# Projections of K, V, Q and gate as fills between the attention tiles of each head, with a lookahead of two tiles in place of three

## What is computed

```python
s = jnp.einsum('bqhd,bkhd->bhqk', qi, k).astype(jnp.float32) * scale
s = s + ci[..., :, None] - cum[:, :, None, :]          # cum = cumsum(log_sigmoid(f))
s = jnp.where(k_pos[None, :] <= pi[:, None], s, NEG_INF)
p = jax.nn.softmax(s, axis=-1).astype(v.dtype)
o = jnp.einsum('bhqk,bkhd->bqhd', p, v)                # prompt; o_fox
...
y_fox = jnp.einsum('btc,cd->btd', o_fox * jax.nn.silu(g_fox), w_fox_out)
```

## Time and profile before

| | |
|---|---|
| median of 2 runs | 4568.74 us |
| the two runs | 4312.99 and 4824.48 us |
| the profiled execution, its own time | 4312.71 us |
| its span on the slowest core | 4311.1 us |
| spans of the eight cores | 4266.9 to 4311.1 us |
| mean granted TensorE clock of the cores | 0.936 to 0.940 |
| TensorE busy | 3636.3 us, 84% |
| VectorE, ScalarE, GpSimd busy | 832.6, 990.1, 806.7 us |

### The profile page before, as it was taken

How to read it: one execution, slowest core, us unless ns; L and a number is a source line. 1 busy time by engine, 2 the same in 40 slices (tenths; PEclk the granted TensorE clock), 3 DMA queues, 4 the chain that set the end, 5 groups by cost and what they waited for, 6 DMA issues and landing times.

```text
span 4311.1 us, 57458 instructions; the slowest of 8 cores (4266.9 to 4311.1 us)
## 1 busy us (share of the span) xinstructions
PE 3636.3 (84%) x20854; PEld 1846.9 (43%) x20854; DVE 832.6 (19%) x1331; ACT 990.1 (23%) x1808; POOL 806.7 (19%) x695
## 2 busy tenths in 40 slices
PE   3888888888888799988999996799958887888598
PEld 2555555555554344433444443344423333333243
DVE  1122222222222211111111111011101112111155
ACT  1344444444444411111111110011111221111011
POOL 1111111111111100001322232122211102222233
PEclk9999999999999899998999998899969998999799
DMA  6533333333333144435244444655492105655853
GB/s 91 70 55 55 51 49 52 51 55 55 55 51 51 20 80 79 86 59 42 27 38 40 40 40 2 103 118 118 109 151 38 20 1 102 131 126 132 172 157 122
DMA packets 500442, 311.75 MB, mean 72 GB/s; under 512 B 275440, under 2 KB 449264, under 8 KB 494140
## 3 DMA queue, kind: packets, MB, share of 16 engines
q0 software_dynamic: 354640, 143.19, 30.1%
q1 hardware_dynamic: 145528, 164.89, 13.8%
HBM read 353.68 MB, written 97.53 MB: 105 GB/s over the span
## 4 chain that ended last, share of the span: by engine, by line
PE 65%; DMA 17%; ACT 5%; issue 4%; POOL 4%; DVE 3%; SPq 1%; DVEq 0%; ACTq 0%; POOLq 0%
PE bank L153 64%; DMA pv<-m_scr 10%; POOL mt L182 3%; ACT pt L170 2%; DMA wm<-w_merge 2%; ACT rl L170 1%; DVE mrl L903 1%; DVE st L192 1%; DMA mwb<-w_mem_kv 1%; SPq L161 1%; DMA xb<-xp 1%; DMA cwb<-w_in 1%; DMA mT<-m_scr 1%; PE bank L157 1%; DMA mwb<-w_in 1%
## 5 line engine op out<-in xcount | busy, mean ns | idle before, releaser
L153 PE MATMUL bank<-xT,wm 128*128 128x512 bf16 (+1 forms) x3840 | 742.1, 347 | 102.0 <-DMA wm<-w_merge 102.0
L153 PE MATMUL bank<-xT,cwb 128*128 128x512 bf16 (+1 forms) x3840 | 693.1, 343 | 44.5 <-DMA cwb<-w_in 36.6
L153 PEld LDWEIGHTS bank<-xT,wm 128*128 128x128 bf16 x3840 | 330.7, 99 | 478.7 <-issue 126.8
L153 PEld LDWEIGHTS bank<-xT,cwb 128*128 128x128 bf16 x3840 | 324.4, 98 | 413.3 <-issue 54.8
L192 DVE SCALAR_TENSOR_TENSOR st<-bank,cqb 128x512 f32<-128x512 f32 (+5 forms) x588 | 295.0, 535 | 908.5 <-PE bank L153 871.8
L153 PE MATMUL bank<-wbuf,xT 128*128 128x256 bf16 (+1 forms) x3264 | 389.6, 283 | 16.4 <-ACT kv L176 16.4
L170 ACT ACTIVATE gt<-bank,bm 128x512 f32<-128x512 f32 (+1 forms) x240 | 147.0, 613 | 1061.7 <-PE bank L153 891.8
L182 DVE TENSOR_TENSOR mt<-bank,gt 128x512 f32<-128x512 f32 (+1 forms) x240 | 143.6, 598 | 1187.4 <-PE bank L153 598.8
L153 PE MATMUL bank<-xT,wbuf 128*128 128x512 bf16 (+1 forms) x1920 | 348.5, 342 | 18.0 <-ACT kT L176 8.5
L153 PEld LDWEIGHTS bank<-wbuf,xT 128*128 128x128 bf16 (+1 forms) x3264 | 330.3, 102 | 70.2 <-issue 21.7
L170 ACT ACTIVATE pt<-st,ncc 128x512 bf16<-128x512 f32 (+5 forms) x588 | 321.8, 594 | 144.0 <-DVE st L192 104.9
(11 more groups left out here) (131 smaller groups left out, 2468.9 us busy)
## 6 DMA issues: line engine op xcount, KB each, us to landing
m_scr<-mt SPq DMA_DIRECT2D x192, 256.0 KB, 2.0
pv<-m_scr SPq DMA_DIRECT2D x128, 256.0 KB, 3.0
wbuf<-w_in POOLq DMA_DIRECT2D x48, 512.0 KB, 12.0
wm<-w_merge POOLq DMA_DIRECT2D x24, 1024.0 KB, 15.1
cwb<-w_in POOLq DMA_DIRECT2D x48, 512.0 KB, 12.6
x<-xp SPq DMA_DIRECT2D x16, 1024.0 KB, 9.2
y_p<-rr SPq DMA_DIRECT2D x16, 1024.0 KB, 5.9
cqb<-cum_scr SPq DMA_DIRECT2D x12, 1024.0 KB, 5.1
```

What stands on the lines that cost most here:

```text
L153: return lambda e: e.matmul(out, lhsT=lhsT, rhs=rhs, start=start, stop=stop)
```

## The change

The projection work of a head is cut into closures: `kv_chunk`, `kv_finish` (casts and stores), `ktrans`, `proj_fm` (Q or gate of one block) and `cache_kT`. For each of the five token blocks there is a list of them in the order K/V chunks, finish, Q, gate, K transpose; the fifth also has the two cache transposes. `issue_S(i)` first emits all that is left of its own block's list, then S, the scale-and-add and Exp, and then one closure of the next block's list (two while in block 0). So block 0's list is emitted in one piece at the head's start, block 1's behind t0 to t3, block 2's behind t4 to t11, block 3's behind t12 to t19, block 4's behind t24 to t30. `load_w(h + 1)` is emitted when block 4's list is empty, behind t30. The lookahead goes from 3 to 2. The score ring has the banks 2, 3, 0 instead of 2, 3, 0, 1, and projections and transposes still alternate between banks 1 and 0.

```diff
+    SRING3 = [2, 3, 0]
+    pjb = [1]
+
+    def next_pj():
+        bk = pjb[0]
+        pjb[0] ^= 1
+        return bk
+
...
-        pending_kt = []
-        for grp in range(5):
-            chunks = [(tc, TCH[tc]) for tc in range(grp * 4, min(grp * 4 + 4, 17))]
-            s = grp % 2
-            for j, (tc, (t0, tn)) in enumerate(chunks):
-                bk = pj[0]; pj[0] ^= 1
+        def kv_chunk(grp, j, tc):
+            def f():
+                t0, tn = TCH[tc]
+                s = grp % 2
+                bk = next_pj()
                 for c in range(16):
-                    S.add(PE, MM(banks[bk][0:tn, 0:256], xT[:, c, t0:t0 + tn],
-                                 wbuf[:, c, 128:384], c == 0, c == 15),
+                    S.add(PE, MM(banks[bk][0:tn, 0:256], xT[:, c, t0:t0 + tn], wbuf[:, c, 128:384], c == 0, c == 15),
                           reads=[r_w[1], r_xT[tc]], writes=[bankr[bk]])
-                S.add(ACT, COPY(kv32[s][0:tn, j, :], banks[bk][0:tn, 0:256]),
-                      reads=[bankr[bk]], writes=[r_kv32[s]])
-            nj = len(chunks)
-            tn = chunks[0][1][1]
-            t0 = chunks[0][1][0]
...
-            def ktrans(grp=grp, s=s, nj=nj, tn=tn, t0=t0):
-                bk = pj[0]; pj[0] ^= 1
+                S.add(ACT, COPY(kv32[s][0:tn, j, :], banks[bk][0:tn, 0:256]), reads=[bankr[bk]], writes=[r_kv32[s]])
...
+        def ktrans(grp):
+            def f():
+                s = grp % 2
+                nj = min(4, 17 - grp * 4)
+                t0, tn = TCH[grp * 4]
+                bk = next_pj()
                 bv = banks[bk].bitcast(BF16)
                 for j in range(nj):
                     S.add(PE, TR(bv[:, j * 128:j * 128 + tn], kb[s][0:tn, j, :], identb[0:tn, 0:tn]),
                           reads=[r_kb[s], r_const], writes=[bankr[bk]])
                 S.add(ACT, COPY(kT[:, t0:t0 + nj * tn], bv[:, 0:nj * 128] if tn == 128 else bv[:, 0:tn]),
                       reads=[bankr[bk]], writes=[r_kT[grp]])
-            if pending_kt:
-                pending_kt.pop()()
-            pending_kt.append(ktrans)
-        for comp, dst, rr, slot in ((0, qT, r_qT, 0), (3, sg, r_sg, 2)):
-            for tb, (t0, tn) in enumerate(TBLK):
-                if tb == 1 and pending_kt:
-                    pending_kt.pop()()
-                bk = pj[0]; pj[0] ^= 1
+            return f
...
+        def proj_fm(comp, tb):
+            def f():
+                t0, tn = TBLK[tb]
+                slot = 0 if comp == 0 else 2
+                bk = next_pj()
...
-        if h + 1 < nheads:
-            load_w(h + 1)
-        for half in range(2):
-            bk = pj[0]; pj[0] ^= 1
-            bv = banks[bk].bitcast(BF16)
-            for j in range(4):
...
+        def cache_kT(half):
+            def f():
+                bk = next_pj()
+                bv = banks[bk].bitcast(BF16)
+                for j in range(4):
...
+        fq = {}
+        for b_ in range(5):
+            q_ = []
+            for j, tc in enumerate(range(b_ * 4, min(b_ * 4 + 4, 17))):
+                q_.append(kv_chunk(b_, j, tc))
+            q_.append(kv_finish(b_))
+            q_.append(proj_fm(0, b_))
+            q_.append(proj_fm(3, b_))
+            q_.append(ktrans(b_))
+            fq[b_] = q_
+        fq[4] += [cache_kT(0), cache_kT(1)]
+        wl = [False]
+
+        def pop_fill(b_, n):
+            if b_ not in fq:
+                return
+            for _ in range(n):
+                if fq[b_]:
+                    fq[b_].pop(0)()
+            if b_ == 4 and not fq[4] and not wl[0]:
+                wl[0] = True
+                if h + 1 < nheads:
+                    load_w(h + 1)
...
-        LA = 3
+        LA = 2
         slots = {}
...
-            sb_ = SRING[sbk[0] % 4]; sbk[0] += 1
+            pop_fill(tbidx, 99)
+            sb_ = SRING3[sbk[0] % 3]; sbk[0] += 1
...
             S.add(ACT, ACTF(pt[p][0:kn, n0:qn], stmp[st][0:kn, n0:qn], AF.Exp, bias=bias),
                   reads=[r_st[st], r_ncc], writes=[r_pt[p]])
+            pop_fill(tbidx + 1, 2 if tbidx == 0 else 1)
...
             if i + LA < nt_:
                 issue_S(i + LA)
             issue_PV(i)
+        for b_ in range(5):
+            pop_fill(b_, 99)
         if h + 1 < nheads:
             load_cache(h + 1)
             load_cqb(h + 1)
```

More of the change, by code:

```diff
@@ L516, in ktrans, with kv_finish @@
-            def ktrans(grp=grp, s=s, nj=nj, tn=tn, t0=t0):
-                bk = pj[0]; pj[0] ^= 1
+                S.add(ACT, COPY(kv32[s][0:tn, j, :], banks[bk][0:tn, 0:256]), reads=[bankr[bk]], writes=[r_kv32[s]])
+            return f
+        def kv_finish(grp):
+            def f():
+                s = grp % 2
+                nj = min(4, 17 - grp * 4)
+                t0, tn = TCH[grp * 4]
+                S.add(POOL, COPY(kb[s][0:tn, 0:nj, :], kv32[s][0:tn, 0:nj, 0:128]), reads=[r_kv32[s]], writes=[r_kb[s]])
+                S.add(POOL, COPY(vb[0:tn, grp * 4:grp * 4 + nj, :], kv32[s][0:tn, 0:nj, 128:256]),
+                      reads=[r_kv32[s]], writes=[r_vb[grp]])
+                if grp < 4:
+                    S.add(SP, DMA(O["fk_p"][t0:t0 + 512, h * 128:(h + 1) * 128].rearrange("(c p) n -> p c n", p=128),
+                                  kv32[s][:, :, 0:128]), reads=[r_kv32[s]], dmasem=d_kvo[s])
+                    S.add(SP, DMA(O["fv_p"][t0:t0 + 512, h * 128:(h + 1) * 128].rearrange("(c p) n -> p c n", p=128),
+                                  kv32[s][:, :, 128:256]), reads=[r_kv32[s]], dmasem=d_kvo[s])
+                else:
+                    S.add(SP, DMA(O["fk_s"][:, h * 128:(h + 1) * 128], kv32[s][0:NS, 0, 0:128]),
+                          reads=[r_kv32[s]], dmasem=d_kvo[s])
+                    S.add(SP, DMA(O["fv_s"][:, h * 128:(h + 1) * 128], kv32[s][0:NS, 0, 128:256]),
+                          reads=[r_kv32[s]], dmasem=d_kvo[s])
+            return f
@@ L532, in build @@
                 for c in range(16):
-                    S.add(PE, MM(banks[bk][:, 0:tn], wbuf[:, c, comp * 128:(comp + 1) * 128], xT[:, c, t0:t0 + tn], c == 0, c == 15),
-                          reads=[r_w[slot]] + xT_res(t0, tn), writes=[bankr[bk]])
+                    S.add(PE, MM(banks[bk][:, 0:tn], wbuf[:, c, comp * 128:(comp + 1) * 128], xT[:, c, t0:t0 + tn],
+                                 c == 0, c == 15), reads=[r_w[slot]] + xT_res(t0, tn), writes=[bankr[bk]])
                 if comp == 0:
-                    S.add(ACT, COPY(dst[:, t0:t0 + tn], banks[bk][:, 0:tn]), reads=[bankr[bk]], writes=[rr[tb]])
+                    S.add(ACT, COPY(qT[:, t0:t0 + tn], banks[bk][:, 0:tn]), reads=[bankr[bk]], writes=[r_qT[tb]])
@@ L537, in build @@
                 else:
-                    S.add(ACT, ACTF(dst[:, t0:t0 + tn], banks[bk][:, 0:tn], AF.Silu), reads=[bankr[bk]], writes=[rr[tb]])
-        if h + 1 < nheads:
-            load_w(h + 1)
-        for half in range(2):
-            bk = pj[0]; pj[0] ^= 1
-            bv = banks[bk].bitcast(BF16)
-            for j in range(4):
-                S.add(PE, TR(bv[:, j * 128:(j + 1) * 128], kc_tm[:, half * 4 + j, :], identb[:, :]),
-                      reads=[r_cache, r_const], writes=[bankr[bk]])
-            S.add(ACT, COPY(kcT[:, half * 512:(half + 1) * 512], bv[:, 0:512]), reads=[bankr[bk]], writes=[r_kcT])
+                    S.add(ACT, ACTF(sg[:, t0:t0 + tn], banks[bk][:, 0:tn], AF.Silu), reads=[bankr[bk]], writes=[r_sg[tb]])
@@ new lines, in proj_fm, with f @@
+            return f
+        def cache_kT(half):
+            def f():
+                bk = next_pj()
+                bv = banks[bk].bitcast(BF16)
+                for j in range(4):
+                    S.add(PE, TR(bv[:, j * 128:(j + 1) * 128], kc_tm[:, half * 4 + j, :], identb[:, :]),
+                          reads=[r_cache, r_const], writes=[bankr[bk]])
+                S.add(ACT, COPY(kcT[:, half * 512:(half + 1) * 512], bv[:, 0:512]), reads=[bankr[bk]], writes=[r_kcT])
+            return f
```

## The result

The changed kernel is slower: 1.0251 of the time before, 95% interval 1.0207 to 1.0295. Its profiled execution took 4417.1 us against 4312.7. In some executions of either kernel the cores of one die show a lower granted clock and take longer; the ratio leaves these out, and the medians over all executions (4459.65 against 4328.27) lie a little further apart.

The account below looks back on a forecast made before the run. TensorE was taken as the bound, 84% busy. Per head, 84.4 us of work, 30.7 of waits and 8 of slow clock made 123.1, 10 more than 113.1; over twelve heads this gave 4430 us, range 4300 to 4530.

Parts of the forecast that it names:

- the likeliest case: The forecast's own outcome: slower, 4430 us in all (its own range 4380 to 4490), chance 0.52.
- Part 1: Waits at ends of query blocks 0 and 1, at head starts and for copies go: 12.3 us a head removed.
- Part 2: Silu between Exps makes 10 table loads a head, not 2; TensorE stalls 2.45, 2.1, 3.35, 2.5 and 6.3 us by block.
- part 4: Bank 0 shared by score tiles and fills: fills wait 4.1 us, score matmuls 1.4, together 5.5 us a head.
- The sign that the prediction named: If right, TensorE waits 2 to 3.4 us for kT's copy before tiles t0, t4 and t12.
- Part 3: Lookahead 2 without fills, from t32 to the head's end: 1.3, 1.55 and 5.6 us (one more than before) a head.
- Block 4's 6.3 us: Silu and table loads falling on the end of block 2: TensorE takes 13.2 us for 6.9 of work.
- Part 5: Next head's weights, loaded later into a single buffer, land before the head ends: cost 0, cover 4 us.
- Part 6: TensorE's time lost to slow clock falls from 11.3 to about 8 us a head.
- A: Faster: fills cover the table switches; a head of 106 us, 4228 us in all; chance 0.13.
- B: No change: bank collisions cost half and the clock recovers 3 us more; 4360 us, chance 0.22.
- C: Weights land 5 us after the head's end and the clock falls; +6 us a head, 4500 us, chance 0.13.

## Why the sum came out, and which of its terms did not

The time, 4417 us against the predicted 4430, and the head, 122.5 against 123.1, are as forecast, and the likeliest case is the one that came. But the sum stands on terms that erred both ways and cancelled, and that is luck.

*Part 1* holds in the main: the waits for `pt` fell by 96 us, and those for K/V copies by 5. The lump at the end of block 3 stayed, as the prediction had it. One lump comes back in part: in one head of three the fill behind S of t14 waits 3.0 us in bank 0 for a scale-and-add that stands behind block 1's end. This part was not tested by itself.

*Part 2* is right at t0 (2.49 against 2.45 us, in every head) and wrong at t4 and t12. It charged 2.1 and 3.35 us in every head because S there would need the K block just transposed. It doesn't. S of t4 waits 2.06 us for kT only in the heads whose ring puts it in bank 0, 0.7 a head, and S of t12 never waits for kT. So 5.45 us of the sum have no ground, and what such waits there are belong to part 4. The sign that the prediction named, waits of 2 to 3.4 us for kT, came true in size (2.49, 2.06, 3.33, 2.63) but after t4 at t20 and t21, not at t12. Order (4.5 us a head) and tables (4.4) were measured with the bank still shared; with the bank and the lookahead mended, order is worth 4.2 and tables about 2.

*Part 3* is near. It gave the shorter lookahead 3.85 us a head (1.3, 1.55 and one for the tail). Measured are 2.8 in the changed kernel, 3.7 with two score banks and 7.8 in the kernel before. The spacing in the unfilled tiles is 1.00 for 1.02.

*Part 4* is the term that failed: 5.5 us a head, measured 10.6 net (the two-bank ring). Fills behind an S in bank 0 wait 6.5 us a head for VectorE (65.9 and 12.7 us over twelve), where 4.1 were priced. What the walk through the queues left out is the other direction, S behind a fill in bank 0: priced at 1.4, it is 9.0 (the 108.6 us). The prediction took the reader's own time, 0.2 us for a copy and more for Silu. In truth the copy stands in ScalarE's queue behind whatever was emitted before it: behind Silu and its table load for a K transpose, and at a block's end behind the whole chain of Ln, Exp, `on`, scale-and-add and Exp, 4.32 us at t27. The three lengths of a head show 6 us between the ways in which the rings meet. Too little by 5.1 us here and too much by 5.45 in part 2 nearly cancel.

Block 4's 6.3 us in part 2 are the same case. TensorE's waits for copies and the scale-and-add from t26 to t31 are 6.4 us a head, but with score banks of their own only 3.6: some 2.8 of them are the shared bank, so the 6.3 came out by another chain than the one walked.

*Part 5* holds for the changed kernel: 2.5 us of waiting in twelve heads. That a shorter tail couldn't be used without an earlier load came true in part, with 11.6 us of waits once a head was down to 104, and single waits of 9.4 and 16.9 us in two other runs.

*Part 6* was too hopeful. It had the part above full speed fall from 11.3 to 8 us a head. TensorE's busy time less the 84.4 us is 12.3 instead (10.8 before over all heads), and the granted clock in the stretch fell from 0.93 to 0.92. Since 84.4 is an estimate, not all of the 12.3 need be clock. Idle time is 25.9 for 30.7, and the two differences, 4.3 more and 4.8 less, also cancel.

Of the rivals, A (the fills cover the switches) fell with the result, and B (bank collisions at half price) with the two-bank ring: the collisions cost twice the price, not half. C didn't come in the changed kernel.

The Trainium skill (ScalarE: Activation LUTs, "What ACT_TABLE_LOAD costs") adds a drain to the table load; in this trace Silu starts 1.29 us after the load does, so none shows. What the Trainium skill advises (same page, "Table sets: the hidden batching unit"), to batch by table set, is worth about 2 us a head here once the order and the banks are right. The larger part of what the loads did was to what was queued behind them.

## What to carry to other kernels

Work that is interleaved to fill one engine's gaps brings its copies into the other engines' queues, and its buffers into the ring of the work that it fills: give it banks of its own before anything else, and emit what the next step needs ahead of what may come later. A reader of such a diff should price each shared buffer by what is queued before its reader, not by the reader's own duration. Where a kernel's units vary with the phase of two rings (49 tiles over three banks), the lengths of single units show the collision at a glance.

## What was not expected of the hardware

That a fill costs so little in itself: with its side costs gone the same matmuls, interleaved, ran at a granted clock of 0.96 in the heads against 0.93 in the kernel before, and a head came within 16.3 us of the estimated 84.4 us of bare work. And the weights' landing spread widely with four loads in a row, from 6.8 to 34.4 us with a median of 15.2 in the changed kernel. There TensorE waited at most 1.9 us at a time for them; in two of the experiments a single late load held it for 9.4 and for 16.9 us.
